# Differential attention: the join one tile later, its ratio on GpSimd, one minimum per tile, a half turn inside the next scores

## What is computed

```python
def diff_attn_core(q, k, v, lam):
    s = jnp.einsum('bhiqd,bhikd->bhiqk', q, k).astype(jnp.float32) * (q.shape[-1] ** -0.5)
    p = jax.nn.softmax(s, axis=-1)
    a = (p[:, :, 0] - lam * p[:, :, 1]).astype(v.dtype)
    return jnp.einsum('bhqk,bhkd->bhqd', a, v)
```

## Time and profile before

| | us |
|---|---|
| median of 3 runs | 1704.83 |
| lowest and highest run | 1698.69, 1709.62 |
| the profiled execution's own time | 1700.46 |
| its span in the trace | 1698.7 |
| busy in the span: TensorE, VectorE, ScalarE, GpSimd | 1630.6, 889.7, 521.2, 600.3 |
| first scores of the stage; first matmul of the output projection | 1142.5, 1271.78 |

### The profile page before, as it was taken

One profiled execution on the slowest core, in us unless ns is written; L12 is line 12 of the kernel. 1 busy time (PEld: TensorE's weight loads), 2 busy tenths in 40 slices (PEclk: granted clock), 3 DMA queues, 4 the chain that ended last, 5 costly groups with the idle time before them and its releaser, 6 DMA issues.

```text
span 1698.7 us, 23785 instructions
## 1 busy us (share of the span) xinstructions
PE 1630.6 (96%) x9326; PEld 1365.3 (80%) x9326; DVE 889.7 (52%) x1176; ACT 521.2 (31%) x924; POOL 600.3 (35%) x353
## 2 busy tenths in 40 slices
PE   5899989999999999999999899999999999999997
PEld 2777878888888888888888788777857888888886
DVE  2400207627963771773685657319964843435264
ACT  3422327525111211211122411128852522222221
POOL 1321247324322332332332333344502644444441
PEclk9899999999999999999999999999999999999998
DMA  9354111311342252333232032200001222222221
GB/s 365 144 213 178 62 63 58 119 57 63 110 163 77 85 174 74 99 120 127 81 119 100 23 115 78 73 25 1 11 29 63 88 100 94 98 94 99 93 81 50
DMA packets 49483, 163.96 MB, mean 97 GB/s; under 512 B 6376, under 2 KB 6632, under 8 KB 45808
## 3 DMA queue, kind: packets, MB, share of 16 engines
q1 hardware_dynamic: 49392, 162.68, 27.7%
HBM read 159.77 MB, written 2.10 MB: 95 GB/s over the span
## 4 chain that ended last, share of the span: by engine, by line
PE 84%; DVE 7%; issue 3%; ACT 2%; DMA 2%; POOL 1%; SPq 0%; DVEq 0%; ACTq 0%; POOLq 0%
PE ps L1467 24%; PE ps L1468 23%; PE ps L1469 23%; PE ps L1900 2%; PE ps L1862 2%; PE ps L1889 1%; PE ps L1775 1%; DVE tmp_a L1126 1%; DVE h L1133 1%; PE ps L1765 1%; DVE mod_acc L1039 1%; PE ps L1653 1%; PE ps L1803 1%; DMA xc<-ctx_dram 1%; POOL h L545 1%
## 5 line engine op out<-in xcount | busy, mean ns | idle before, releaser
L533 POOL TENSOR_TENSOR w_lo<-raw,w_hi 128x1024 fp32r<-128x1024 f32 x189 | 468.8, 2484 | 923.3 <-ACT w_hi L680 923.1
L1467 PE MATMUL ps<-h,w_hi 128*128 128x512 f32 (+1 forms) x1168 | 414.7, 355 | 15.4 <-DVE h L1133 4.9
L1468 PE MATMUL ps<-h,w_lo 128*128 128x512 f32 (+1 forms) x1168 | 412.2, 353 | 0.0
L1469 PE MATMUL ps<-h,w_hi 128*128 128x512 f32 (+1 forms) x1168 | 409.5, 351 | 0.0
L680 ACT ACTIVATE w_hi<-raw 128x1024 fp32r<-128x1024 f32 x189 | 199.8, 1057 | 429.1 <-PE ps L1469 403.0
L1467 PE MATMUL ps<-hid_lo,w_hi 128*128 128x512 f32 (+1 forms) x800 | 279.4, 349 | 0.5 <-DVE hid_lo L1219 0.5
L1468 PE MATMUL ps<-hid_hi,w_lo 128*128 128x512 f32 (+1 forms) x800 | 278.8, 349 | 0.0
L1469 PE MATMUL ps<-hid_hi,w_hi 128*128 128x512 f32 (+1 forms) x800 | 277.2, 347 | 0.0
L1467 PEld LDWEIGHTS ps<-h,w_hi 128*128 128x128 f32 x1168 | 222.7, 191 | 57.1 <-issue 11.7
L1469 PEld LDWEIGHTS ps<-h,w_hi 128*128 128x128 f32 x1168 | 221.8, 190 | 30.8
L1468 PEld LDWEIGHTS ps<-h,w_lo 128*128 128x128 f32 x1168 | 222.5, 190 | 28.8
(11 more groups left out here) (203 smaller groups left out, 2176.9 us busy)
## 6 DMA issues: line engine op xcount, KB each, us to landing
raw<-units_dram SPq DMA_DIRECT2D x189, 512.0 KB, 3.3
mod_ring<-w_mod_dram SPq DMA_DIRECT2D x96, 256.0 KB, 3.2
mod_big<-w_mod_dram SPq DMA_DIRECT2D x16, 1024.0 KB, 8.7
mod_late<-w_mod_dram SPq DMA_DIRECT2D x8, 1024.0 KB, 6.1
xl<-x_dram SPq DMA_DIRECT2D x2, 2048.0 KB, 11.6
bias<-bias_dram SPq DMA_DIRECT2D x8, 384.0 KB, 3.8
xc<-ctx_dram SPq DMA_DIRECT2D x2, 1024.0 KB, 13.6
out_dram<-out_t SPq DMA_DIRECT2D x8, 256.0 KB, 2.9
```

Of the source, the lines that this page charges most:

```text
L533: nc.gpsimd.tensor_tensor(w_lo[:, s], raw[:, s], w_hi[:, s].bitcast(F32), op=ALU.subtract).then_inc(lo_made, 1)
L1467: mm(out, a[0], b[1], start=start, stop=False)
L1468: mm(out, a[1], b[0], start=False, stop=False)
L1469: return mm(out, a[0], b[0], start=False, stop=stop)
```

## The change

- VectorE: the two minima of a tile are one reduction over both maps, giving two columns. The reciprocal (`inverse1`) stays; the product with the first sum and lambda goes to GpSimd. The join of tile n-1 now comes after the reciprocal of tile n and before the minimum of tile n+2.
- GpSimd: `ratio(n)` in each tile; the splits of the next head are spread over the tiles (casts after ratio 4h+3, key lows after the next, query lows after the one after that), and the squares too.
- TensorE: the first half turn of tile n-1 is issued in the middle of scores n+2 (after 6 of its 12 matmuls); the second half turn of tile n-1 comes after the weigh. The sums of squares are regrouped: heads 0 to 5 in the last pass, head 6 after it.
- ScalarE: in pass n the order is turned n-3 half 1, exponential n map 0, turned n-2 half 0, exponential n map 1.

```diff
+            def ratio(n):
+                pool.wait_ge(inv1, n + 1)
+                nc.gpsimd.tensor_scalar(stat[:, 28 + n % 3:29 + n % 3], stat[:, 32 + n % 3:33 + n % 3], lam_t[:, 4:5],
+                                        l_first[:, n:n + 1], ALU.mult, ALU.mult).then_inc(r1, 1)
...
-            for h in range(HEADS):
-                if h + 1 < HEADS:
-                    if h:
-                        pool.wait_ge(s1, 8 * h)
-                        keys_high1(h + 1)
-                    queries_high1(h + 1)
-                    keys_low1(h + 1)
-                    queries_low1(h + 1)
-                if h:
-                    out_square(2 * h - 2)
-                    out_square(2 * h - 1)
+            queries_high1(1)
+            for n in range(4 * HEADS):
+                ratio(n)
+                h = (n + 1) // 4 + 1
+                if h < HEADS:
+                    if n % 4 == 3:
+                        pool.wait_ge(s1, 8 * (h - 1))
+                        keys_high1(h)
+                        queries_high1(h)
+                    elif n % 4 == 0:
+                        keys_low1(h, 0)
+                        keys_low1(h, 1)
+                    elif n % 4 == 1:
+                        queries_low1(h, 0)
+                        queries_low1(h, 1)
+                if n >= 6 and n % 2 == 0:
+                    out_square(n // 2 - 3)
+            out_square(2 * HEADS - 3)
...
             def exps(n, i):
-                act.wait_ge(m1, 2 * n + 2)
+                act.wait_ge(m1, n + 1)
...
-                for i in range(2):
-                    if 2 <= n <= N1 + 1:
-                        turned1(n - 2, i)
-                    if n < N1:
-                        exps(n, i)
+                if 3 <= n <= N1 + 2:
+                    turned1(n - 3, 1)
+                if n < N1:
+                    exps(n, 0)
+                if 2 <= n <= N1 + 1:
+                    turned1(n - 2, 0)
+                if n < N1:
+                    exps(n, 1)
...
             def least1(n):
-                for i in range(2):
-                    dve.wait_ge(s1, 2 * n + 2)
-                    c = 16 + 2 * (n % 2) + i
-                    V.tensor_reduce(stat[:, c:c + 1], scores_ps(n)[:, TOK * i:TOK * i + TOK], AX.X, ALU.min).then_inc(m1, 1)
-
-            def ratio(n):
+                dve.wait_ge(s1, 2 * n + 2)
+                c = 16 + 2 * (n % 2)
+                V.tensor_reduce(stat[:, c:c + 2], scores_ps(n).rearrange("p (i k) -> p i k", i=2), AX.X, ALU.min).then_inc(m1, 1)
+
+            def inverse1(n):
                 dve.wait_ge(e1, 2 * n + 2)
-                c, d = 22 + n % 3, 28 + 2 * (n % 3)
-                st.wait(V.reciprocal(stat[:, d:d + 1], stat[:, c:c + 1]))
-                st.wait(V.tensor_scalar(stat[:, d + 1:d + 2], stat[:, d:d + 1], lam_t[:, 4:5], l_first[:, n:n + 1],
-                                        ALU.mult, ALU.mult))
+                V.reciprocal(stat[:, 32 + n % 3:33 + n % 3], stat[:, 22 + n % 3:23 + n % 3]).then_inc(inv1, 1)
 
             def combine(n):
-                d = 29 + 2 * (n % 3)
+                dve.wait_ge(r1, n + 1)
+                d = 28 + n % 3
...
-            for n in range(N1):
-                ratio(n)
-                combine(n)
+            for n in range(N1 + 1):
+                if n < N1:
+                    inverse1(n)
+                if n:
+                    combine(n - 1)
                 if n + 2 < N1:
                     least1(n + 2)
...
                 score(1, outer[1], 1)
                 score(0, outer[0], 0)
+                if between:
+                    between()
                 score(1, outer[1], 2)
                 score(0, outer[0], 1)
...
                 if n + 2 < N1:
-                    scores1(n + 2)
-                if n >= 1:
-                    turn1(n - 1, 1)
+                    scores1(n + 2, (lambda: turn1(n - 1, 0)) if n else None)
+                else:
+                    turn1(n - 1, 0)
                 if n >= 3:
                     weigh1((n - 3) // 2, (n - 3) % 2)
-                if n == N1 - 1:
+                if n == N1:
                     pe.wait_ge(oneh_in, 32)
-                    for h in range(4):
+                    for h in range(HEADS - 2):
                         sub_sums(h)
-                if n == N1:
-                    for h in range(4, HEADS - 1):
-                        sub_sums(h)
-                if n < N1:
-                    turn1(n, 0)
+                if n:
+                    turn1(n - 1, 1)
+            sub_sums(HEADS - 2)
```

More of the change, by code:

```diff
@@ L326, in build @@
         first_in = sem("first_in")
+        inv1 = sem("inv1")
+        r1 = sem("r1")
         m1 = sem("m1")
@@ L627, in queries_high1, with keys_low1, queries_low1 @@
                 nc.gpsimd.tensor_copy(aqh[h % 2][:], q1[:, h]).then_inc(qh1, 1)
[L629 to L641, removed]
+            def keys_low1(h, piece):
+                if piece == 0:
+                    pool.wait_ge(kh1, h + 1)
+                sl = slice(384 * piece, 384 * piece + 384)
+                ins = nc.gpsimd.tensor_tensor(akl[h % 2][:, sl], k1[:, h, sl], akh[h % 2][:, sl].bitcast(F32), op=ALU.subtract)
+                if piece:
+                    ins.then_inc(kl1, 1)
+            def queries_low1(h, piece):
+                if piece == 0:
+                    pool.wait_ge(qh1, h + 1)
+                sl = slice(256 * piece, 256 * piece + 256)
+                ins = nc.gpsimd.tensor_tensor(aql[h % 2][:, sl], q1[:, h, sl], aqh[h % 2][:, sl].bitcast(F32), op=ALU.subtract)
+                if piece:
+                    ins.then_inc(ql1, 1)
             def out_square(m):
@@ L652, in _ @@
             queries_high1(0)
-            keys_low1(0)
-            queries_low1(0)
+            for piece in range(2):
+                keys_low1(0, piece)
+            for piece in range(2):
+                queries_low1(0, piece)
             lows(FIRST["out1"] - 1, FIRST["out1"])
             pool.wait_ge(lo_made, FIRST["out1"] + AHEAD)
-            for h in range(HEADS):
-                if h + 1 < HEADS:
-                    if h:
-                        pool.wait_ge(s1, 8 * h)
-                        keys_high1(h + 1)
-                    queries_high1(h + 1)
-                    keys_low1(h + 1)
-                    queries_low1(h + 1)
-                if h:
-                    out_square(2 * h - 2)
-                    out_square(2 * h - 1)
+            queries_high1(1)
[16 more added lines that the diff above has]
+            out_square(2 * HEADS - 3)
             lows(FIRST["out1"], FIRST["mlp1"])
@@ L992, in _ @@
             for n in range(N1 + 4):
-                for i in range(2):
-                    if 2 <= n <= N1 + 1:
-                        turned1(n - 2, i)
-                    if n < N1:
-                        exps(n, i)
+                if 3 <= n <= N1 + 2:
[6 more added lines that the diff above has]
+                    exps(n, 1)
                 if n >= 5 and n % 2 == 1:
                     out_copy((n - 5) // 2)
-                if n == N1 + 1:
+                if n == N1 + 2:
                     act.wait_ge(sub_mm, 1)
@@ L1415, in _ @@
             least1(1)
-            for n in range(N1):
-                ratio(n)
-                combine(n)
+            for n in range(N1 + 1):
[3 more added lines that the diff above has]
+                    combine(n - 1)
                 if n + 2 < N1:
                     least1(n + 2)
-                if n == N1 - 3:
+                if n == N1 - 2:
                     eps_terms(0, N1 - 4)
-                if n == N1 - 1:
+                if n == N1:
                     eps_terms(N1 - 4, N1)
@@ L1843, in _, with scores1 @@
                            (lambda n: pe.wait_ge(v1_out, n + 1)) if j == 1 and i == 0 else None)
-            def scores1(n):
+            def scores1(n, between=None):
                 h, p = n // 4, n // 4 % 2
```

## The result

The changed kernel takes 1731.12 us (median of 4 runs, 1730.42 to 1735.47), the kernel before 1701.76 us (median of 4 runs, 1698.26 to 1709.62); the ratio is 1.0168, with a 95% interval of 1.0141 to 1.0195. The forecast was 1731 us, 26.4 us above the median of then; the measured distance is 29.4 us. The profiled execution has a span of 1728.6 us, 29.9 more than before.

What follows compares the result with a forecast made beforehand. It took TensorE to bound the attention stage at 3.35 us a tile; a new VectorE-TensorE loop of 4.20 us, over 28 rounds plus the ending, adds 26.4 us: 1704.83 + 26.4 = 1731 us, 8-in-10 range 1719 to 1744.

Steps and rivals of the forecast that it cites:

- What bounds the kernel before: Differential attention: TensorE sets the pace with four pieces, 3.35 us a tile; VectorE works almost without idle time beside it.
- The round: VectorE and TensorE take turns per tile (join, turn, second half of scores, minimum, reciprocal): 4.20 us against 3.35, chance 0.83.
- The join's term: VectorE's join in the loop: 1.10 us, between 1.02 undisturbed and 1.17 on the mean with GpSimd beside it.
- The stage: Differential attention, some 115 us of the span: the change costs 26.4 us there; following stages keep their length.
- The sum behind the loop: From the end of join 28 to the stage's end: last weigh ends 22.2 us later, output projection starts 28.6 later.
- The step that failed: TensorE's scores split by the turn: 0.2 us more a tile, 3.55 us alone, bounds 3.35 and 3.65.
- rival 1: TensorE keeps the pace, only its longer work counts: 29 x 0.2 = 6 us, 1711 us; chance 0.09.
- Rival 3: TensorE's clock falls in the stage: some 12 more rounds of 0.9, 11 us, 1742 us; chance 0.05.
- Rival 2: VectorE sets today's 3.35 us, its relief comes through on 29 tiles: 11 us faster, 1694 us; chance 0.03.
- rival 4: The change doesn't do what it says, GpSimd's ratio late by a tile; chance less than 0.02.

Runs made afterwards that it cites:

- experiment 1: Changed kernel with the first half turn behind all twelve scores instead of after six: 1703.94 us, ratio 1.0011 to the kernel before.
- experiment 6: Kernel before with one change alone, the two minima of a tile as one instruction: 1702.72 us, ratio 1.0009.
- experiment 3: Changed kernel with join n directly after reciprocal n and the ratio back on VectorE, turn still mid-scores: 1719.09 us, ratio 1.0096.
- experiment 4: Changed kernel with the join in two instructions of 384 columns, the first half turn waiting for the first only: 1717.3 us, ratio 1.0078.
- experiment 5: Changed kernel with the ratio back on VectorE between reciprocal n and join n-1: 1741.34 us, ratio 1.0247.
- experiment 9: Changed kernel with the turn behind all scores, plus a lone identity transpose after three of twelve scores: 1718.58 us, ratio 1.0111.
- experiment 10: Changed kernel with five more matmuls of 512 columns in TensorE's wait at the stage's end: 1729.32 us, ratio 1.0169.
- experiment 8: Changed kernel with the turn behind all scores, plus a lone identity transpose in the middle of the scores: 1722.25 us, ratio 1.0117.
- experiment 7: Changed kernel with the turn behind all scores and join n directly after reciprocal n, ratio still on GpSimd: 1713.79 us, ratio 1.0058.

## Why the prediction was right, point by point

- **What bounds the kernel before.** TensorE's four pieces at 3.35 us, with VectorE full but not in charge. Shown by experiments 1 and 6: with VectorE relieved, the spacing stays 3.35 and the time the same.
- **The round.** It decides, and it has the predicted members. Breaking it by moving the turn (experiment 1), by the order on VectorE (3) or by the size of the join (4) makes the kernel faster by 27, 12 and 14 us by the medians, and the stage alone, from the first scores to the first spread in the profiles, shorter by 22.9, 12.0 and 7.4; putting 0.3 us into it (5) makes the kernel slower by 10 and the stage longer by 11.5. (The stages of 4 and 5 have 13.7 us at 1.2 GHz at their start, which makes them longer.)
- **Its size:** 4.17 us, forecast 4.20. The sum hides errors that cancel. Too high were the join (1.10 for 1.00 to 1.01) and the reciprocal (0.17 for 0.07: the join no longer waits for the result of the instruction before it). Too low were the turn (0.42 for 0.48), the second half of the scores (0.47 for 0.58) and the minimum (1.66 for 1.68). That 4.17 lies so near 4.20 is luck in part. The 0.11 of the second half was in the prediction: it priced one step more of 0.115 us for TensorE's own work and left it out of the round.
- **The join's term** was wrong in kind, not only in size. It kept half of the old disturbance by GpSimd. In the new order reciprocal n releases GpSimd just after join n-1 has started, so GpSimd is the one held up, and the join runs undisturbed: mean 1011 ns for 1168.
- **The stage:** 27.0 us longer, forecast 26.4. The sum behind the loop holds too: the last weigh ends 22.4 us after join 28 (1268.6 to 1291.0 us in the chain), forecast 22.2. VectorE waits 44.8 us, where the prediction had 30 to 40; TensorE's matmuls show 0.24 us before a first half turn and not 0.6 to 0.8, since the split's own cost had taken much of the gap.
- **The step that failed**, though the forecast came true: "I estimate 0.1 for that, so TensorE alone would need about 3.35 + 0.2 = 3.55 us a tile, bounds 3.35 and 3.65". It measured 3.86. The change between 64-row and 128-row work was priced at 0.1; experiment 3 shows 0.32 in the two halves of the scores and 0.19 at the weigh behind them. It did not decide the pace, because 3.86 is still below 4.17, and what it put into the round (0.06 at the turn, 0.11 at the second half) was offset by the join and the reciprocal. But rival 1 would have ended at 1701.8 + 29 x 0.51 = 1717 us and not at 1711, and the margin to the round was 0.3 us, not 0.65. "TensorEngine Tiling (Array Packing)" of the Trainium skill, Key Properties, says that changing the mode drains the engine; the traces agree in that a break and its return cost 0.36 us beyond the inserted work (experiment 9).
- **The distance, 29.4 for 26.4 us:** the median of the kernel before moved from 1704.83 to 1701.76 with one more run, so that the forecast time of 1731 fits better than the forecast step. In the profiled executions 27.0 - 1.3 + 4.2 make the 29.9, and the 4.2 is the longer stretch at 1.2 GHz behind the stage. Rival 3 looked for it inside the stage. There the clock fell only once, at the start, for 3.4 us from 1160 on; the turns beside it are 5.56 us apart instead of 4.17 (1159.00 and 1164.56 in the chain), which is 1.4 of the 27.0 us. The profiles of experiments 4, 5 and 10 had 13.7 us at the lower clock there; in experiment 10 two rounds then took 5.06 and 5.10 us instead of 4.17 (minima at 1149.15, 1154.21 and 1159.31 in its chain), which is the 0.9 a round that rival 3 named. So its price was right; the stretches were short and stood only at the stage's start.
- **Rival 2** fell with experiments 1 and 6; **rival 4** with 0.2 us of waiting for the ratio.

No variant beat the kernel before: with TensorE in charge at 3.35 us a tile, orders that don't shorten its own work can only keep or lose.

## What to carry to other kernels

Before moving an instruction that waits into the middle of a block, follow one round: who waits for the end of the block, and is the releaser queued behind that waiter on its own engine? If so, two engines take turns, and the sum of the round's members, from start to start, is the new pace, however much slack each engine shows. Compare that sum with the engines' own floors, since the larger one rules and they do not add up; and look whether the chain of waits passes through an engine before relieving it: here relief of one at 98% gained nothing that could be measured.

## What the runs showed of the hardware

- An interruption of 64-row matmuls in pairs by 128-row work costs TensorE about 0.36 us beyond the inserted work, and another 0.11 us when the two halves of the array have had 256 columns more on one side (3.93, 3.82 and 3.35 us a tile in experiments 8, 9 and 1).
- A one-column product on GpSimd takes 0.34 us alone and 1.03 us when VectorE's join has started just before it; the join of 768 columns takes 1.01 us on the mean when it starts first and 1.46 us when GpSimd does (experiment 7).
- One minimum over 1536 elements of PSUM took 1758 ns, two over 768 took 947 each; by starts that is 1.68 against 1.73 us, so joining them saves only 0.05 us.
- Behind the stage TensorE's clock was at 1.2 GHz for 3.4 to 23.9 us in the twelve profiled executions, and the rest of the kernel took 430.3 to 440.2 us with it. The kernel before had 3.4 us and experiment 6 had 13.7, with the same matmuls ahead of it.
